# First attention: GpSimd splits two of the eight chunks of turned probabilities of each unit

## The reference, cut to what matters

```
def blocked_gqa(q, k, v):
    # q (B,T,8,64), k and v (B,T,2,64); blocks of 128 queries
    s = einsum('bqkgd,bskd->bkgqs', qblk, k)
    p = softmax(s, axis=-1)
    return einsum('bkgqs,bskd->bqkgd', p, v)
```

## Time and profile before

| | us |
|---|---|
| median of 3 runs | 2482.29 |
| lowest and highest of them | 2481.96, 2482.37 |
| the profiled execution, by its own clock | 2479.31 |
| its span in the profile | 2477.5 |
| PE busy in the span | 2344.5 (95%) |
| DVE busy | 1117.5 (45%) |
| ACT busy | 775.9 (31%) |
| POOL busy | 860.2 (35%) |
| mean granted TensorE clock, share of full speed | 0.982 |

### The profile page before, as it was taken

One profiled execution on the slowest core, in us unless ns is written; L12 is line 12 of the kernel. 1 busy time (PEld: TensorE's weight loads), 2 busy tenths in 40 slices (PEclk: granted clock), 3 DMA queues, 4 the chain that ended last, 5 costly groups with the idle time before them and its releaser, 6 DMA issues.

```text
span 2477.5 us, 30786 instructions
## 1 busy us (share of the span) xinstructions
PE 2344.5 (95%) x11310; PEld 1925.1 (78%) x11310; DVE 1117.5 (45%) x1381; ACT 775.9 (31%) x1096; POOL 860.2 (35%) x851
## 2 busy tenths in 40 slices
PE   4897888999999999999999999999999999999997
PEld 3676777777888888888777888887778888888886
DVE  7958888478641344124463334353211122222324
ACT  3216777123320222023424445462122111112220
POOL 1345554225423333323233323232223334333331
PEclk9998999999999999999999999999999999999999
DMA  7311000623211111111131111102011111111132
GB/s 303 111 38 43 17 17 10 255 102 131 89 51 51 43 51 51 43 60 51 38 115 63 39 53 51 39 30 83 30 36 45 51 51 51 51 47 38 51 127 77
DMA packets 48318, 166.02 MB, mean 67 GB/s; under 512 B 4480, under 2 KB 6272, under 8 KB 48128
## 3 DMA queue, kind: packets, MB, share of 16 engines
q1 hardware_dynamic: 48256, 165.19, 19.4%
HBM read 156.79 MB, written 8.39 MB: 67 GB/s over the span
## 4 chain that ended last, share of the span: by engine, by line
PE 80%; DVE 9%; issue 4%; ACT 4%; POOL 1%; DMA 1%; SPq 0%; DVEq 0%; ACTq 0%; POOLq 0%
PE acc L747 62%; PE turn L972 6%; PE bank L1036 3%; DVE ADA L1656 1%; PE bank L1014 1%; PE acc L960 1%; DVE HL L1636 1%; DVE acc L1812 1%; PE turn L641 1%; PE bank L849 1%; ACT EX L1259 1%; PE acc L725 1%; DMA ADA<-in_ada 1%; PE bank L1111 1%; PE bank L1108 1%
## 5 line engine op out<-in xcount | busy, mean ns | idle before, releaser
L747 PE MATMUL acc<-HH,WH 128*128 128x512 f32 x1600 | 498.3, 393 | 16.0 <-POOL WL L541 15.1
L747 PE MATMUL acc<-HL,WH 128*128 128x512 f32 x1600 | 495.0, 391 | 0.0
L747 PE MATMUL acc<-HH,WL 128*128 128x512 f32 x1600 | 494.1, 390 | 0.0
L538 POOL TENSOR_TENSOR WH<-WF,CON 128x16 fp32r<-128x16 f32 x186 | 49.5, 266 | 1224.1 <-PE acc L747 1009.4
L541 POOL TENSOR_TENSOR WL<-WF,WH 128x1024 fp32r<-128x1024 f32 (+2 forms) x186 | 441.3, 2372 | 15.5
L747 PEld LDWEIGHTS acc<-HH,WH 128*128 128x128 f32 x1600 | 301.0, 189 | 82.3 <-POOL WL L541 13.0
L747 PEld LDWEIGHTS acc<-HL,WH 128*128 128x128 f32 x1600 | 301.9, 189 | 63.3
L747 PEld LDWEIGHTS acc<-HH,WL 128*128 128x128 f32 x1600 | 301.6, 189 | 63.1
L539 POOL TENSOR_SCALAR WH<-WF 128x1008 fp32r<-128x1008 f32 (+2 forms) x186 | 192.5, 1035 | 0.0
L1942 DVE SCALAR_TENSOR_TENSOR CV<-EV,VEC,CV 128x1023 f32<-128x1023 f32 x44 | 99.1, 2251 | 204.0 <-ACT CV L1335 203.3
L1870 DVE SCALAR_TENSOR_TENSOR XT<-acc,MOD,XT 128x1024 f32 (+1 forms) x34 | 43.6, 1284 | 233.0 <-PE acc L747 233.0
(11 more groups left out here) (374 smaller groups left out, 4104.2 us busy)
## 6 DMA issues: line engine op xcount, KB each, us to landing
WF<-in_w SPq DMA_DIRECT2D x150, 512.0 KB, 3.3
ADA<-in_ada SPq DMA_DIRECT2D x15, 1024.0 KB, 14.8
BIAS<-in_bias SPq DMA_DIRECT2D x16, 576.0 KB, 3.8
XT<-in_xT SPq DMA_DIRECT2D x16, 512.0 KB, 10.0
ADA<-in_ada SPq DMA_DIRECT2D x4, 2048.0 KB, 11.8
ADA<-in_ada SPq DMA_DIRECT2D x3, 2560.0 KB, 9.2
WF<-in_w SPq DMA_DIRECT2D x24, 256.0 KB, 2.6
ADA<-in_ada SPq DMA_DIRECT2D x8, 512.0 KB, 3.3
```

The source lines that it names most:

```text
L538: pool.tensor_tensor(h[:, 0:FEW], f[:, 0:FEW], zero.to_broadcast([P, FEW]), ALU.add).then_inc(w_hi, 1)
L747: last = pe.matmul(acc[:, slot, HALF * c:HALF * c + HALF], w[slot][:, k, :], x[:, k, HALF * c:HALF * c + HALF], start=(k == 0 and w is WH ...
```

## The change

A new SBUF buffer `PTF` holds two slots of 128 x 256 float32. Of the eight chunks of a unit, chunks 6 and 7 (the last two of half h1) take another way:

- ScalarE copies them from PSUM to `PTF` in float32 (new instruction, 256 columns), and its copy of h1 to `PTH` shrinks from 512 to 256 columns. It waits on the new semaphore `ptp_ready` before it overwrites a slot, that is until GpSimd has finished with the unit two before.
- VectorE's low part of h1 shrinks from 512 to 256 columns.
- GpSimd gets a function `split_probs(it, u)`: it adds zero to `PTF` and writes the high part to `PTH`, waits for that, and subtracts it from `PTF` into `PTL`; two instructions of 256 columns. It waits for `pth_ready` of unit u's h1. The call stands behind the step of `stack_queries` of the same unit, where there is one, and ahead of the `ML` of unit 12.
- TensorE's `values` waits on `ptp_ready` at k = 6, until both units of the pair have been split.
- One instruction on one column at GpSimd's start of the stage sets `ptp_ready` to 4.

```
@@ GpSimd
+            def split_probs(it, u):
+                pool.wait_ge(pth_ready, it * 32 + (2 * u + 2))
+                f, h = PTF[:, u % 2, :, :], PTH[:, 6:8, u % 4, :]
+                pool.tensor_tensor(h, f, zero.unsqueeze(2).to_broadcast([P, 2, P]), ALU.add).then_inc(ptp_ready, 1)
+                pool.wait_ge(ptp_ready, it * 32 + (2 * u + 5))
+                pool.tensor_tensor(PTL[:, 6:8, u % 4, :], f, h.bitcast(F32), ALU.subtract).then_inc(ptp_ready, 1)
...
                     if 9 <= u <= 11 and not last:
                         stack_queries(it, 2, u - 9, it * 32 + (2 * u + 4))
+                    split_probs(it, u)
                     if u == 12:
...
+            pool.tensor_tensor(PTF[:, 0, 0, 0:1], zero, zero, ALU.add).then_inc(ptp_ready, 4)
@@ TensorE, values
+                        if k == 6:
+                            pe.wait_ge(ptp_ready, now + 6)
@@ ScalarE
-                        act.activation(PTH[:, 4 * h:4 * h + 4, u % 4, :],
-                                       turns[(2 * u + h) % 3].rearrange("p (k q) -> p k q", q=P), ACT.Copy
-                                       ).then_inc(pth_ready, 1)
+                        x = turns[(2 * u + h) % 3].rearrange("p (k q) -> p k q", q=P)
+                        n = 4 - 2 * h
+                        if h == 1:
+                            act.wait_ge(ptp_ready, it * 32 + (2 * u + 2))
+                            act.activation(PTF[:, u % 2, :, :], x[:, 2:4, :], ACT.Copy)
+                        act.activation(PTH[:, 4 * h:4 * h + n, u % 4, :], x[:, 0:n, :], ACT.Copy).then_inc(pth_ready, 1)
@@ VectorE
+                        ks = slice(4 * h, 4 + 2 * h)
+                        dve.tensor_tensor(PTL[:, ks, u % 4, :],
+                                          turns[(2 * u + h) % 3].rearrange("p (k q) -> p k q", q=P)[:, 0:4 - 2 * h, :],
+                                          PTH[:, ks, u % 4, :].bitcast(F32), ALU.subtract).then_inc(ptl_ready, 1)
```

More of the change, by code:

```diff
@@ L159, in build @@
         PTL = at("PTL", 48, [P, TT, 4, P], F32R)
+        PTF = at("PTF", 84, [P, 2, 2, P])
         EX = [at(f"EX{s}", kb, [P, T]) for s, kb in enumerate((64, 68, 16, 20))]
@@ L299, in build @@
             sem("scores_done"), sem("nb_ready"), sem("exp_done"), sem("rc_ready"), sem("exn_ready"))
+        ptp_ready = sem("ptp_ready")
         pt_done, pth_ready, ptl_ready, pv_done, otmp_ready, o_ready, mh_ready, ml_ready = (
@@ L1841, in attend @@
                         dve.wait_ge(pth_ready, it * 32 + (2 * u + h + 1))
-                        dve.tensor_tensor(PTL[:, 4 * h:4 * h + 4, u % 4, :],
-                                          turns[(2 * u + h) % 3].rearrange("p (k q) -> p k q", q=P),
-                                          PTH[:, 4 * h:4 * h + 4, u % 4, :].bitcast(F32), ALU.subtract).then_inc(ptl_ready, 1)
+                        ks = slice(4 * h, 4 + 2 * h)
+                        dve.tensor_tensor(PTL[:, ks, u % 4, :],
+                                          turns[(2 * u + h) % 3].rearrange("p (k q) -> p k q", q=P)[:, 0:4 - 2 * h, :],
+                                          PTH[:, ks, u % 4, :].bitcast(F32), ALU.subtract).then_inc(ptl_ready, 1)
                     if u % 8 == 5:
```

## The result

| | before | after |
|---|---|---|
| median, us | 2482.12 | 2507.93 |
| lowest and highest | 2481.24, 2482.37 | 2502.74, 2511.69 |
| runs | 4 | 4 |
| the profiled execution | 2479.31 | 2508.20 |
| its span | 2477.5 | 2506.2 |

The ratio after to before is 1.0103, 95% interval 1.0088 to 1.0118: 1.0% slower. Of the 28.7 us between the two spans 24.9 lie in the first attention (start of the first normalise to start of the last ML), 3.8 elsewhere.

What follows compares the result with a forecast made beforehand. The prediction took a loop of largest, exponentials and inverse to bound ordinary units, and GpSimd's chain the groups; -3.2 + 21.4 + 2.4 + 2.4 = +23.0 us gave a median of 2505.3 us, range 2493 to 2516.

Steps and rivals of the forecast that it cites:

- The bound: Ordinary units: a loop of largest, exponentials and inverse sets 2.84 us a unit, not VectorE, so they neither gain nor lose.
- The price of a split: GpSimd's two instructions of 256 columns: 0.61 us add, 0.74 subtract, with wait and overlap 1.38; 1.23 to 1.51.
- ScalarE's copies: One copy of 0.594 us becomes two of at most 0.399, hidden in ordinary units, 0.05 us a group.
- A group: Behind stack_queries' steps, two splits between QL and normalise +2.76, values' wait +0.25, ScalarE +0.05: +3.06 us, seven times.
- Units 5, 9, 13: VectorE's low parts are on the path there; shorter by 0.27 us each, 12 places, -3.2 us.
- The tail: Behind the second group, GpSimd's queue with ML makes normalise 14 about 0.7 us late, three times, +2.1 us.
- The port: In units 5 VectorE's product of two SBUF tiles waits for the split: +0.6 us, four times, +2.4 us.
- The last iteration: It has one group at +3.06 us; at its end unit 15's split replaces a VectorE low part, +0.3 us.
- The rest of the program: Everything outside the first attention stays as long as before; what lies behind the stage only shifts.
- a bound on VectorE: Rival: low parts are on the path in every unit, 17 us come off, 2465 us; chance 0.03.
- cover in the groups: Rival: GpSimd's idle time absorbs the groups' splits, about +2 us, 2484 us; chance 0.05.
- The lower clock: Rival: longer TensorE stops cost each of seven groups 2 us more at 1.2 GHz, +14, 2519 us; chance 0.12.

Runs made afterwards that it cites:

- e4: Before, with VectorE's low part of h1 on 256 columns and the low parts of chunks 6 and 7 left out of the output; 2482.93 us, ratio 1.0003.
- e5: Before, with ScalarE's copy of half h1 to PTH made as two copies of 256 columns, nothing else changed; 2481.79 us, ratio 1.0003.
- e7b: After, with the splits only in units 5 and 13; 2482.95 us, ratio to before 1.0008.
- e10: After, with ML of unit 12 put ahead of the split of unit 12 on GpSimd; 2504.88 us, ratio to before 1.0094.
- e2: Before, with the same two GpSimd instructions on an unused buffer behind each step of stack_queries, other engines unchanged; 2507.27 us, ratio 1.0110.
- e9: After, with splits of units 1 and 9 ahead of QL, those of 2, 3, 10, 11 behind the normalise TensorE waits for; 2499.74 us, ratio to before 1.0078.
- e11: After, with the changed GpSimd orders of e9 and e10 together; 2498.38 us, ratio to before 1.0064.

## Why the prediction was right, point by point

The median came out at 2507.93 us for 2505.3 forecast, slower, by the mechanism named. That the two are so near is in part luck: several terms were off by about 1 us each and cancelled in part, as the sum below shows, and by the profiled execution the forecast was 2502.3 for 2508.20 measured.

- **The bound.** Right. Ordinary intervals stayed at 2.84, and e4 shows that VectorE's busy share named the wrong engine.
- **The price of a split.** 1.38 forecast, 1.37 measured: add 0.61 us, subtract 0.73. The value for the add rested on the row of QST, and it was the right row. By the figure for two-input work in the GPSIMD Engine Reference of the Trainium skill (section 3.1) the add would cost as much as the subtract, and a split an estimated 1.51 us; for an add with a broadcast operand the trace does not agree.
- **ScalarE's copies.** 0.38 and 0.39 us, hidden; e5 puts the whole at nothing in ordinary units.
- **A group.** +3.06 forecast; the first measured +3.08, of which 2.73 is QL to normalise and 0.26 the values' wait at k = 6.
- **The second group.** 13 and 15 are longer by 1.28 and 2.14, 3.42 together, of which 0.27 gives back the gain of 12 (e4 does the same); 3.15 remain.
- **Units 5, 9, 13.** Oversized. The forecast took -0.27 at twelve places, -3.2 us. That of unit 9 is given back one interval later. What can be kept are the places of units 5 and 13, as e7b shows in each iteration, and in after even these are spent: unit 5's on the port (4.50 for 4.52), unit 13's in the tail.
- **The tail.** 0.7 a group forecast. Interval 16 is 0.55 longer although the low part is 0.27 shorter, so about 0.8. Its cause was only half named: it is not only normalise 14 that comes late but the gather of unit 13, which waited 0.68 us for ML. The prediction did not see that wait.
- **The port.** It does hold VectorE up, but less: +0.6 forecast, 1.45 us instead of 1.22 measured, +0.23, since only the second instruction of the split was still at work when the product began (unit 5 of after, GpSimd and VectorE):

```profile
239.37 0.73 POOL L581 TENSOR_TENSOR PTL<-PTF,PTH 128x256 fp32r<-128x256 f32 x1
```

```profile
239.73 1.45 DVE L1673 SCALAR_TENSOR_TENSOR ADA<-ADA,C1B 128x1024 f32<-128x1024 f32 x1
```

  In unit 13 of the last iteration, where the prediction had VectorE first, the subtract started 0.04 us ahead of the product (450.33 and 450.37), and the product took 1.79: there the 0.6 was right and the place was not. Where GpSimd came second it was the one that paid, 1.77 us for 0.73. With the rule of the Trainium skill (SBUF — State Buffer, "Who interferes with whom") both rows agree: the first holds the port to its end; and beside low parts, which read PSUM, the splits ran at 0.73.
- **The last iteration.** +3.15 forecast, +4.03 measured (QL to ML 46.58 and 50.61). Most of the difference is a stretch at the lower clock, shown below: from the last largest to ML after took 13.63 us, e10 with a clock of 1.00 there took 12.83, and before took 12.57.
- **The rest of the program.** "All else as long as before" failed by 3.8 us in the profiled run. The table of versions says how to take that: the rest is between 2256.9 and 2261.8 us in twelve other executions, none of which touches it, and e4 with a shorter stage has the longest. It is the scatter of single executions, not a cost that this change alone shows; the medians differ by 25.8 us, 0.9 more than the stage.

The sum: +23.0 forecast for the stage, +24.9 measured. Three iterations by QL to QL gave 20.8 for 19.8, the last 4.0 for 3.15. Against the forecast stand, in the three iterations, +0.8 for unit 9's gain given back, -1.1 for the port, +0.4 for the tail and +0.3 in the groups; +0.9 in the last iteration; and some 0.6 in tenths where iterations meet (2.90 for 2.84).

Of the rivals, a bound on VectorE falls with e4, and cover in the groups falls with the largest of unit 7 at 12.38 us. The lower clock is real but small in after; e2 shows that it was near, since four of its seven groups lost about 1.5 us each to it. What was not named is that GpSimd, once behind in a group, has next to no idle time left to catch up, which e9 and e11 show as the limit of the better orders tried.

## What to carry to other kernels

Work moved to an idle engine is free only where that engine is idle within the loop that bounds; look for the few places where it already works without a gap, count what new instructions stand there between an input and the result that others wait for, and multiply. If the order can be changed, put the new work behind that result, but first add up the engine's work up to the next place where others wait for it: when it nears the time there is, the debt comes back at that place. A gain of some tenths at a place where another engine's step comes next should be counted only when the interval after it is seen not to grow.

## What the runs showed of the hardware

**The lower clock comes in one group and not in another.** In the first group of after, stops of 1.98 us in the values of units 0 and 1 and of 1.76 us ahead of the turn left the clock at 1.00. In the last iteration it fell. The turn ahead of it, then matmuls of 256 columns that start 0.22 us apart instead of 0.12, and the stretch:

```profile
449.74 0.66 PE L878 MATMUL turn<-CON,EX 128*128 128x128 f32 x4 [1.95 <-POOL EX L573]
...
451.14 0.41 PE L863 MATMUL bank<-PTH,VTOK 128*128 128x256 f32 x1
451.36 0.41 PE L863 MATMUL bank<-PTL,VTOK 128*128 128x256 f32 x1
```

```profile
450.00:455.00 5.00, 5.00 (x32) 4.84 (x30) 3.15 (x7) 1.38 (x4) 3.60 (x6) 0.66 0.00 0
```

A waiting TensorE so can pay twice, once for the wait and once for some microseconds at 1.2 GHz behind it. Which stops bring it on can't be told from these rows: e10 had a stop of 1.96 us ahead of the same turn, and its granted clock stayed at 1.00 from 443 to 461 us.

**A chain far behind the change.** In the large products of after a tile of weights was split late: TensorE stood for 3.08 us and then ran partly at the lower clock. GpSimd's first instruction on that tile, its low part and the matmul that waited, then the stretch:

```profile
653.69 1.12 POOL L540 TENSOR_TENSOR WH<-WF,CON 128x16 fp32r<-128x16 f32 x1 [12.06 <-DMA WF<-in_w]
...
656.87 3.19 POOL L543 TENSOR_TENSOR WL<-WF,WH 128x1024 fp32r<-128x1024 f32 x1
...
660.19 1.22 PE L759 MATMUL acc<-HH,WH 128*128 128x512 f32 x2 [3.08 <-POOL WL L543]
```

```profile
655.00:668.00 13.00, 9.92 (x32) 7.66 (x31) 12.93 (x10) 3.18 (x3) 11.37 (x5) 0.74 0.14 44
```

The instruction that answers to the first of these in before, to judge by its place in the sequence:

```profile
625.97 0.41 POOL L538 TENSOR_TENSOR WH<-WF,CON 128x16 fp32r<-128x16 f32 x1 [8.43 <-DMA WF<-in_w]
```

In before TensorE had no stop behind it (busy 15.00 of 15.00 us from 630 to 645, clock 1.00). GpSimd waited for the load 12.06 us in after and 8.43 in before, so 3.6 us longer; the instruction itself, beside VectorE's products, took 1.12 us for 0.41, so 0.7 longer. The late load is therefore the larger part. By its time it is the load that SyncE issued at 643.49, behind another at 642.75 that followed the end of a product of VectorE at 642.72. What made that product late against TensorE's work is open; no run here isolates it.
